# GpSimd makes two of the eight tiles of u before each up-projection, and the sample's factors are applied in two halves

## The reference, cut to what matters

```python
def rmsnorm(x, g):
    xf = x.astype(jnp.float32)
    y = xf * lax.rsqrt(jnp.mean(xf * xf, axis=-1, keepdims=True) + EPS)
    return (y * g.astype(jnp.float32)).astype(x.dtype)

u = rmsnorm(x, ng[0]) * (1.0 + sc1) + sh1
x = x + 0.5 * g1 * swiglu(u, P['w_ffn_up'][l, 0], P['w_ffn_down'][l, 0])
...
u = rmsnorm(x, ng[2]) * (1.0 + sc3) + sh3
x = x + 0.5 * g3 * swiglu(u, P['w_ffn_up'][l, 1], P['w_ffn_down'][l, 1])
```

## Time and profile before

| | |
|---|---|
| median of three runs | 3175.61 us (3175.28 to 3176.03) |
| the profiled execution, its own time | 3176.12 us |
| its span, first to last instruction | 3174.4 us |
| mean granted TensorE clock | 0.998 |
| TensorE busy | 99% of the span |
| VectorE, ScalarE, GpSimd busy | 37%, 13%, 27% |

### The profile page before, as it was taken

One profiled execution on the slowest core, in us unless ns is written; L12 is line 12 of the kernel. 1 busy time (PEld: TensorE's weight loads), 2 busy tenths in 40 slices (PEclk: granted clock), 3 DMA queues, 4 the chain that ended last, 5 costly groups with the idle time before them and its releaser, 6 DMA issues.

```text
span 3174.4 us, 42750 instructions
## 1 busy us (share of the span) xinstructions
PE 3132.2 (99%) x17722; PEld 2483.5 (78%) x17722; DVE 1169.0 (37%) x2229; ACT 421.1 (13%) x806; POOL 856.6 (27%) x749
## 2 busy tenths in 40 slices
PE   7999999999999999999999999999999999999999
PEld 5777887678777878888877778876787778788887
DVE  3223432453233463344232233224533244633432
ACT  2000001212111120000010000023021111200000
POOL 2333431210000334334333334302100003344442
PEclk9999999999999999999999999999999999999999
DMA  6544323541111223332234443234311113222221
GB/s 244 196 174 171 127 74 107 161 136 40 51 51 58 90 79 115 112 112 81 86 120 170 176 169 116 74 119 147 126 53 51 34 58 106 77 80 80 80 83 65
DMA packets 73504, 337.43 MB, mean 106 GB/s; under 512 B 10592, under 2 KB 27744, under 8 KB 40288
## 3 DMA queue, kind: packets, MB, share of 16 engines
q1 hardware_dynamic: 63936, 312.03, 27.1%
q0 software_dynamic: 6816, 18.88, 2.0%
q10 hardware_dynamic: 2560, 3.80, 0.3%
HBM read 326.55 MB, written 6.02 MB: 105 GB/s over the span
## 4 chain that ended last, share of the span: by engine, by line
PE 97%; DVE 2%; ACT 1%; DMA 1%; issue 0%; SPq 0%; DVEq 0%; ACTq 0%
PE ps L702 96%; DVE ws L1729 1%; ACT ws L1450 0%; DMA lp<-params 0%; ACT u L1450 0%; DMA ring<-w_ada 0%; DVE u L1729 0%; DVE proj L1729 0%; DVE masked_room L2104 0%; PE ps L762 0%; DVE x L1732 0%; PE ps L1277 0%; DVE masked_room L1729 0%; DVE masked_room L1732 0%; PE ps L1164 0%
## 5 line engine op out<-in xcount | busy, mean ns | idle before, releaser
L702 PE MATMUL ps<-u,ring 128*128 128x272 f32 x4608 | 1145.4, 398 | 10.9 <-ACT u L1450 9.3
L702 PEld LDWEIGHTS ps<-u,ring 128*128 128x128 f32 x4608 | 858.1, 190 | 227.3 <-issue 45.6
L1729 DVE TENSOR_TENSOR ws<-ws,ps 128x272 f32<-128x272 f32 (+2 forms) x778 | 346.6, 451 | 1488.9 <-PE ps L702 1482.1
L665 POOL TENSOR_TENSOR masked_room<-ring 128x512 f32<-128x512 f32 (+1 forms) x76 | 95.8, 1260 | 1277.9 <-DVE pause L2430 651.6
L702 PE MATMUL ps<-y,ring 128*128 128x272 f32 x1376 | 350.8, 393 | 0.0
L1450 ACT ACTIVATE ws<-ps 128x272 f32<-128x272 f32 (+1 forms) x398 | 154.9, 396 | 1316.0 <-PE ps L702 1315.4
L702 PE MATMUL ps<-y,masked_room 128*128 128x272 f32 x1296 | 315.9, 393 | 2.8 <-DVE ws L1729 2.8
L702 PE MATMUL ps<-y,ws 128*128 128x272 f32 x1296 | 315.7, 393 | 0.0
L702 PEld LDWEIGHTS ps<-y,ring 128*128 128x128 f32 x1376 | 261.4, 190 | 54.3 <-DVE proj L1729 0.7
L702 PEld LDWEIGHTS ps<-y,masked_room 128*128 128x128 f32 x1296 | 245.6, 190 | 55.7 <-issue 5.3
L702 PEld LDWEIGHTS ps<-y,ws 128*128 128x128 f32 x1296 | 246.0, 190 | 51.9 <-issue 1.6
(11 more groups left out here) (201 smaller groups left out, 2543.4 us busy)
## 6 DMA issues: line engine op xcount, KB each, us to landing
ring<-w_up SPq DMA_DIRECT2D x88, 1024.0 KB, 4.8
ring<-w_ada SPq DMA_DIRECT2D x72, 1024.0 KB, 4.8
ring<-w_down SPq DMA_DIRECT2D x32, 1024.0 KB, 4.7
ring<-w_gate SPq DMA_DIRECT2D x32, 1024.0 KB, 4.8
ring<-w_in SPq DMA_DIRECT2D x22, 1024.0 KB, 4.8
ws<-cache SPq DMA_DIRECT2D x128, 128.0 KB, 3.1
ws<-cache POOLq DMA_DIRECT2D x128, 128.0 KB, 3.4
ring<-w_down SPq DMA_DIRECT2D x16, 768.0 KB, 4.1
```

What stands on the lines that cost most here:

```text
L665: nc.gpsimd.tensor_tensor(sums[:, 0], a21, a22, ALU.add).then_inc(w_sums.sem, 1)
L702: return nc.tensor.matmul(out, lhsT, rhs, start=start, stop=stop, skip_group_check=skip)
L1729: return V.tensor_tensor(out, a, b, op)
```

## The change

In the up-projections' norms VectorE makes tiles 0 to 5 of u; GpSimd makes tiles 6 and 7, behind the weight sums of panel 0, and signals them by `un_pool`. ScalarE waits for `un_pool` before tiles 6 and 7. The sample's factors are applied to tiles 0 to 3 before the first token sum and to tiles 4 to 7 after it, each time in two instructions of 128 x 128. The norm of the token mixing is left as it is.

```diff
+VECTOR_U, UN0, US0 = 6, (0, 6, 22), (0, 2, 3)
...
-        un_done = signal("normed", 32)
+        un_done = signal("normed", 2 * VECTOR_U + 16)
+        un_pool = signal("normed_last_tiles", 2 * (KT - VECTOR_U))
...
# GpSimd, weight_sums(f)
                         block_sums(f"up{f}", up_place(l, f, q), unit_of(f"up{f}", q), 4)
+                        if q == 0:
+                            pool.wait_ge(rt_done.sem, rt_done.upto(l, (1, 4)[f]))
+                            for k in range(VECTOR_U, KT):
+                                nc.gpsimd.tensor_tensor(u[:, k, :], x[:, k, :], rs[:, :], ALU.mult)\
+                                    .then_inc(un_pool.sem, 1)
...
# ScalarE, norm(l, n)
-                        act.wait_ge(un_done.sem, un_done.upto(l, U0[n] + 8 * i + k + 1))
+                        if n == 1 or k < VECTOR_U:
+                            act.wait_ge(un_done.sem, un_done.upto(l, UN0[n] + 8 * i + k + 1))
+                        else:
+                            act.wait_ge(un_pool.sem, un_pool.upto(l, (n // 2 + 1) * (KT - VECTOR_U) - KT + k + 1))
...
# VectorE, norm(l, n)
-                    for k in range(KT):
+                    for k in range(KT if n == 1 else VECTOR_U):
                         tt_(u[:, k, a:b], x[:, k, a:b], rs[:, a:b], MUL).then_inc(un_done.sem, 1)
...
-                dve.wait_ge(un_done.sem, un_done.upto(l, U0[n] + (16 if n == 1 else 8)))
-                us = u[:, :, TP:T].rearrange("p k (s t) -> p k s t", s=NSEQ)
+                dve.wait_ge(un_done.sem, un_done.upto(l, UN0[n] + (16 if n == 1 else VECTOR_U)))
+                sample_u(l, n, 0, KT if n == 1 else 4)
+
+            def sample_u(l, n, k0, k1):
+                us = u[:, k0:k1, TP:T].rearrange("p k (s t) -> p k s t", s=NSEQ)
 
                 def by_seq(v):
-                    return v.unsqueeze(3).to_broadcast([P, KT, NSEQ, TD])
-
-                link(l, tt_(us, us, by_seq(mod_a[:, 8 * n:8 * n + 8, 1:9]), MUL))
-                tt_(us, us, by_seq(mod[:, 24 * n:24 * n + 8, 1:9]), ADD).then_inc(us_done.sem, 1)
+                    return v.unsqueeze(3).to_broadcast([P, k1 - k0, NSEQ, TD])
+
+                link(l, tt_(us, us, by_seq(mod_a[:, 8 * n + k0:8 * n + k1, 1:9]), MUL))
+                tt_(us, us, by_seq(mod[:, 24 * n + k0:24 * n + k1, 1:9]), ADD).then_inc(us_done.sem, 1)
...
# VectorE, ffn(l, n)
                 dve.wait_ge(up_done.sem, up_done.upto(l, U0[2 * n] + 4))
-                dve.wait_ge(us_done.sem, us_done.upto(l, 2 * n + 1))
+                dve.wait_ge(us_done.sem, us_done.upto(l, US0[2 * n] + 1))
                 tt_(tsum[:, 0], b12, b11, SUB).then_inc(t_sums.sem, 1)
+                dve.wait_ge(un_pool.sem, un_pool.upto(l, (n + 1) * (KT - VECTOR_U)))
+                sample_u(l, 2 * n, 4, KT)
+                dve.wait_ge(us_done.sem, us_done.upto(l, US0[2 * n] + 2))
                 dve.wait_ge(up_done.sem, up_done.upto(l, U0[2 * n] + 8))
```

More of the change, by code:

```diff
@@ L238, in last_part @@
     return PART0[l][stage] + k
-VEC_LINKS, ACT_LINKS, RW_LINKS = 145, 15, 5
+VEC_LINKS, ACT_LINKS, RW_LINKS = 147, 15, 5
 class Signal:
@@ L488, in build @@
         rt_done = signal("roots", 4)
-        un_done = signal("normed", 32)
+        un_done = signal("normed", 2 * VECTOR_U + 16)
+        un_pool = signal("normed_last_tiles", 2 * (KT - VECTOR_U))
         up_done = signal("u_prompt", 32)
-        us_done = signal("u_sample", 3)
+        us_done = signal("u_sample", 5)
         t_sums = signal("token_sums", 2 * 4)
@@ L1006, in halves_in @@
                             wait_u(l, 1, 16)
-                            pe_.wait_ge(us_done.sem, us_done.upto(l, 2))
+                            pe_.wait_ge(us_done.sem, us_done.upto(l, US0[1] + 1))
                         for k in range(KT):
```

## The result

The changed kernel takes 3189.69 us (median of six runs, 3184.92 to 3190.5) against 3176.57 for the kernel before (3175.28 to 3177.59, six runs of its own): ratio 1.0038, 95% interval 1.0025 to 1.0051, 13.1 us. The forecast was 3183.9, with 3180.2 to 3188.0 as its range: the sign was right, the size was not, and the time lies outside the range.

What follows compares the result with a forecast made beforehand. TensorE, busy 99%, bounds the kernel, with ScalarE slower than VectorE in the norms. Turns 2.1 + 2 x 2.0 + 1.2 plus clock 1.0 make 8.3 us on 3175.6: 3183.9 us, range 3180.2 to 3188.0.

Steps and rivals of the forecast that it cites:

- What bounds the kernel, and that there was nothing to gain: Up-projection norms: ScalarE is slower than VectorE (0.71 against 0.64 us a tile), so relieving VectorE shortens no ScalarE step.
- Whole turns, 1.77 us for a pair: Tiles of u: VectorE and GpSimd instructions alternate whole; one turn of each takes 1.77 us, in which VectorE finishes one tile.
- the other of the two cases: Layer 1, first norm: GpSimd, not VectorE, wins the tie at the start; M6 2.2 us late instead of 2.1.
- The sum of the turns: Delay of M6: 2.1 us in layer 1's first norm, 2.0 in each second norm, 1.2 in layer 0's first.
- The clock, "I take 0.3 a place, + 1.0 in all": TensorE's granted clock falls to half level during stretched waits: 0.3 us a place, 1.0 in all.
- The bound of 1.8 a place: Upper bound of the clock loss: a product of eight takes its 1.84 us twice, 1.8 us a place.
- The sum's own bounds: Total from GpSimd tiles of 1.27 us without clock loss to 1.59 with 1.8 in three places: 6.7 to 14.7 us.
- The clock's rival: Clock stays at half through the products: 3.2 us more in layer 1's first norm, 1.5 each second norm; 3189.1 us, 10%.
- The stream that keeps its turn: VectorE's stream runs on, GpSimd's tiles get in only after tile 5: 3.3 us together, 3178.9 us; 7%.
- No turns between tiles: Tiles of u on both engines do not collide, ScalarE is fed in time everywhere: 3175.6 us, not slower; 5%.
- GpSimd's queue and the panel 1 sums: Panel 1 sums start 1.3 to 2.4 us later behind the third token sum, but are covered: no cost.

Runs made afterwards that it cites:

- the run with zeros: The changed kernel with GpSimd writing zeros into tiles 6 and 7 of u instead of the product, reading nothing from SBUF: 3177.27 us, ratio 1.0001.

## Why the prediction was wrong

**What bounds the kernel, and that there was nothing to gain**: right. ScalarE is the slower engine of the chain, and in the run with zeros, where VectorE is relieved for nothing, its stretch and the time stay.

**Whole turns, 1.77 us for a pair**: right. VectorE's six tiles take 6.20 and 7.51 (forecast 6.17 and 7.49), GpSimd's instruction 1.33 (1.34). In the tie of layer 1's first norm GpSimd is first, the other of the two cases; it had been put at 2.2 and measured 2.0 with the clock held up.

**The sum of the turns**: right, a little high. With the clock held up it is 2.0 + 1.84 + 1.84 in three places (2.1, 2.0, 2.0). At the program's start M6 comes 12.0 us after the turned modulation (the two matmuls at 36.11, 48.14) where it came 10.9 after (36.48, 47.40): 1.1 for the 1.2 forecast. The second profile of the kernel before has 10.3 there, so this one is known to half a microsecond only. (The table has 0.7 there, since the changed kernel's execution reached that modulation 0.4 us earlier.) Together 6.8 for 7.3.

**The clock, "I take 0.3 a place, + 1.0 in all"**: this is the step that failed. It measured 0.6, 1.4 and 2.0, 4.0 us together. I had taken the price from the earlier trace rows, a fall whose low stretch was used up under ScalarE's tiles and before a tie. The bound of 1.8 a place was the nearer one, and not even an upper one: in layer 1's second norm the half level reached from 2756.6 to 2763.4, over two products, and cost 2.0. The reason was in the prediction's own text, k-steps 1.8 us apart, and the low end was taken all the same. The sum's own bounds, 6.7 to 14.7 above, held the result; the stated range ended at 12.4. The clock's rival, with 10%, said 3189.1 and had the place right, with 3.2 and 1.5 each. That it comes within 0.6 us of the result is luck: its 6.2 us of clock measured 4.0, and falls elsewhere that it didn't count made up the difference.

**What was not in the sum at all**: 3.3 us of falls in the mixing stage, near 1002 and 2582. Turns 6.8, clock 4.0 and these 3.3, less the 0.4 of the earlier start and 0.1, are the 13.6 of the two profiles. The prediction took the profile before, where PEclk is 1.00 there, as how the kernel always runs. The kernel before has such a fall too, near 1001 in its second profile, and its times reach 3180 to 3181 in the later comparisons where the first three lay within 0.8 us. Whether the changed kernel has them more often is open: seven of its 13 executions are in the upper group, and profiles are too few to count. The low group alone, 3184.9 to 3186.4, would have lain within the range: that the median of six fell above it is in part chance, the clock term being too small is not.

**The rivals.** The stream that keeps its turn (7%) is out: six tiles would have taken 3.9 us. No turns between tiles (5%) is out. GpSimd's queue and the panel 1 sums, costed at nothing, cost nothing: the stretches between the places are equal to 0.1 us wherever the clock is full.

**Open.** What makes the clock fall in the mixing stage was not found. The guess that the 64 small matmuls do it led to an edit that left the falls in place.

## What to carry to other kernels

Before work is moved from one engine to another beside it, look which engine sets the pace of that chain and whether the two engines' instructions take turns; here the relieved engine was not the pace-setter and the turns cost more than the work moved. If a change stretches the waits between TensorE's matmuls, price the clock at the half level for at least the product that follows them (1.8 us here, where three profiles have 0.6 to 2.1 a place), and compare profiles of several executions before calling a clock reading a property of the kernel. And when GpSimd must work beside VectorE, its position decides: behind the tiles that the next engine is waiting for, the same instructions cost 1.1 us a place in place of 1.84 to 2.0.

## What was not expected of the hardware

- One operand read is enough: a GpSimd copy (0.635 us) makes VectorE's two-operand instruction 0.45 us longer, a write of the same tile (0.55 us) does not lengthen it.
- The half level of the clock comes in executions of one and the same program at places where TensorE is busy 8.00 of 8.00 us (1000 to 1008, PEclk 0.79), and not in others; it is worth 1.6 to 1.7 us each time there, so two of them would be about half of the 6.7 us by which executions of the unchanged kernel differ over three comparisons (3174.64 to 3181.33), an estimate.
- Eleven executions with the clock held up by extra matmuls lie within 1.4 us; the changed kernel's own lie within 6.5.
